# A weight ring of 11 slots in place of 8, square roots in groups of two chunks, and another rstd in the last tile

## The reference

```
xn  = rmsnorm(x);  z = xn @ w_in -> xa, ga, u, v, gates
A:  xc = causal_conv(xa);  r, i = sigmoid(block-diagonal maps of xc)
    log_a = -8 * r * softplus(-lam);  a = exp(log_a);  mult = sqrt(-expm1(2*log_a))
    h = scan(h = a*h + mult*(i*xc));  o_a = (h * gelu(ga)) @ w_br_a
B:  o_b = (gelu(u) * (w_s @ layernorm(gelu(v)) + b_s)) @ w_br_b      (128-position chunks)
mix = (sigmoid(g_a)*o_a + sigmoid(g_b)*o_b) @ w_out;  x += rmsnorm(mix)
f = (silu(gate) * up) @ w_ffn_out, gate/up = rmsnorm(x) @ w_ffn_in;  x += rmsnorm(f)
```

## Time and profile before

| | |
|---|---|
| time, median of 3 runs | 2117.57 us (2116.72 to 2122.35) |
| time of the profiled execution | 2120.24 us |
| its span on the slowest core, core 5 | 2118.5 us |
| spans of the 8 cores | 2103.1 to 2118.5 us |
| TensorE busy on core 5 | 2064.9 us (97%) |
| VectorE, ScalarE, GpSimd busy | 1192.0, 911.3, 359.4 us |
| DMA, mean over the span | 189 GB/s |

### The profile page before, as it was taken

How to read it: one execution, slowest core, us unless ns; L and a number is a source line. 1 busy time by engine, 2 the same in 40 slices (tenths; PEclk the granted TensorE clock), 3 DMA queues, 4 the chain that set the end, 5 groups by cost and what they waited for, 6 DMA issues and landing times.

```text
span 2118.5 us, 34763 instructions; the slowest of 8 cores (2103.1 to 2118.5 us)
## 1 busy us (share of the span) xinstructions
PE 2064.9 (97%) x10771; PEld 1019.9 (48%) x10771; DVE 1192.0 (56%) x1878; ACT 911.3 (43%) x1546; POOL 359.4 (17%) x735
## 2 busy tenths in 40 slices
PE   7999999999999999999999999999999999999997
PEld 3444444444444444444454455445564455445553
DVE  5887488524785257833675168625763587236342
ACT  5667476213761246512752148215822483133111
POOL 3211333113210122001210031003101212121000
PEclk9999999999999999999999999999999999999999
DMA  8655778997478974677554476447666645865652
GB/s 200 140 130 104 206 180 199 186 207 242 159 183 185 236 233 145 184 195 222 199 179 159 153 265 200 159 156 259 210 201 193 230 162 165 257 215 194 212 185 90
DMA packets 113671, 401.43 MB, mean 189 GB/s; under 512 B 14089, under 2 KB 14097, under 8 KB 113490
## 3 DMA queue, kind: packets, MB, share of 16 engines
q1 hardware_dynamic: 96786, 340.43, 48.5%
q0 software_dynamic: 16272, 57.68, 17.1%
q10 hardware_dynamic: 432, 1.09, 0.2%
HBM read 403.26 MB, written 53.54 MB: 216 GB/s over the span
## 4 chain that ended last, share of the span: by engine, by line
PE 89%; DMA 6%; DVE 2%; issue 1%; ACT 1%; SPq 0%; POOL 0%; DVEq 0%; POOLq 0%; ACTq 0%
PE ps L783 62%; PE ps L1376 13%; PE ps L1074 5%; PE ps L1277 5%; DMA wring<-wall 2%; DMA wring<-wsc 2%; PE ps L684 1%; PE ps L964 1%; PE ps L1389 1%; DMA xin<-xp 1%; DVE xcf L946 1%; PE ps L1136 1%; DMA x<-xp 1%; PE ps L1484 0%; DMA yp<-x 0%
## 5 line engine op out<-in xcount | busy, mean ns | idle before, releaser
L783 PE MATMUL ps<-xnT,wring 128*128 128x512 bf16 (+2 forms) x5696 | 1154.3, 359 | 11.7 <-DMA wring<-wall 4.0
L783 PEld LDWEIGHTS ps<-xnT,wring 128*128 128x128 bf16 x5696 | 552.7, 98 | 560.1 <-issue 24.8
L1376 PE MATMUL ps<-wring,ffT 128*128 128x512 bf16 (+1 forms) x1364 | 297.1, 379 | 0.0
L1355 ACT ACTIVATE sgt<-ps 128x512 f32<-128x512 f32 (+2 forms) x198 | 109.4, 555 | 403.4 <-PE ps L783 395.4
L1359 DVE SCALAR_TENSOR_TENSOR sgt<-sgt,ps 128x512 f32<-128x512 f32 (+2 forms) x198 | 125.3, 633 | 213.3 <-PE ps L783 212.9
L1376 PEld LDWEIGHTS ps<-wring,ffT 128*128 128x128 bf16 (+1 forms) x1364 | 132.8, 98 | 162.4 <-issue 4.6
L946 DVE SCALAR_TENSOR_TENSOR xcf<-xa,vecs_sb,xcf 128x512 f32<-128x512 f32 (+2 forms) x240 | 163.4, 681 | 26.7 <-DVE xcf L946 0.9
L1361 DVE SCALAR_TENSOR_TENSOR ffT<-sgt,ps 128x512 bf16<-128x512 f32 (+2 forms) x198 | 125.8, 635 | 39.5 <-PE ps L783 36.4
L500 POOL DMA_DIRECT2D wring<-wall x113 | 63.4, 561 | 445.5 <-PE ps L783 343.4
L656 POOL TENSOR_SCALAR stats<-stats 128x1 f32<-128x1 f32 (+1 forms) x132 | 35.6, 270 | 562.4 <-ACT ffT L669 461.2
L1399 ACT ACTIVATE sgt<-ps 128x512 f32<-128x512 f32 x66 | 38.5, 593 | 197.5 <-PE ps L1376 181.3
(11 more groups left out here) (159 smaller groups left out, 2085.2 us busy)
## 6 DMA issues: line engine op xcount, KB each, us to landing
wring<-wsc SPq DMA_DIRECT2D x473, 512.0 KB, 4.5
wring<-wall POOLq DMA_DIRECT2D x107, 512.0 KB, 9.8
wsc<-wring SPq DMA_DIRECT2D x68, 512.0 KB, 9.4
x<-xp SPq DMA_DIRECT2D x31, 512.0 KB, 7.8
yp<-x SPq DMA_DIRECT2D x29, 512.0 KB, 7.0
xin<-xp SPq DMA_DIRECT2D x28, 512.0 KB, 6.3
wring<-wsc SPq DMA_DIRECT2D x12, 256.0 KB, 3.5
wring<-wall POOLq DMA_DIRECT2D x6, 256.0 KB, 8.5
```

What stands on the lines that cost most here:

```text
L783: mm(lambda e, k=k: e.matmul(ps[:, b, 0:nt], lhsT=wv[:, k, m * 128:(m + 1) * 128], rhs=rhsT[:, k, 0:nt], start=(k == 0), stop=(k == NCH - ...
L1355: act(lambda e: e.activation(out=sgt[:, i, 0:nt], in_=ps[:, b, 0:nt], func=AF.Tanh, scale=0.5), nt, [("ps", b)], [("sgt", i)])
L1376: mm(lambda e, j=j, kk=kk, b=b, PT=PT, col=col: e.matmul(ps[0:PT, b, :], lhsT=ffT[:, j, col:col + PT], rhs=wv[:, kk, :], start=(j == 0), s ...
```

## The change

The ring gets 11 slots, and the scratch area for the DMAs that GpSimd issues is set to 4096 bytes a partition in place of the default. While tile 1's rows are not all squared, at most 8 pieces are loaded ahead. In the pair the 16 places form 8 groups of two square roots, in order of their first place; single tiles keep 4 and 4. In the last tile `fa` adds and takes a reciprocal on VectorE and a square root on ScalarE; the multiplication by the gain becomes a stage of its own, `fg`, after it, and writes to `chE` in place of PSUM.

```diff
-NSLOT = 8
+NSLOT = 11
-    nc = bass.Bass("TRN2", target_bir_lowering=False)
+    nc = bass.Bass("TRN2", target_bir_lowering=False, dynamic_dma_scratch_size=4096)
-                most = 0 if ... else 5 if ("xsq", 0, 3) not in done else len(stream)
+                most = 0 if ... else 5 if ("xsq", 0, 3) not in done else 8 if ("xsq", 1, 3) not in done else len(stream)
+                    if n == "sqrt":
+                        q.extend(sorted(sum(map(list, rest), []), key=lambda z: z.key[2]))
+                        continue
+                sq_from = [0, 2, 4, 6, 8, 10, 12, 14] if M == 2 else [0, 4]
+
                 def sq_of(c):
-                    return -1 if M == 2 and upos(c) < 2 else upos(c) // 4
+                    return max(p for p in sq_from if p <= upos(c))
-                    if upos(c) % 4 == 3 or M == 2 and upos(c) == 1:
-                        put("sqrt", ("sqrt", mem[0], sq_of(c)), lambda c=c: sqrt([GU["ch", i] for i in range(max(0, upos(c) - 3), upos(c) + 1)
-                                                                                   if M == 1 or upos(c) != 3 or i > 1]),
+                    if upos(c) + 1 in sq_from + [M * NCH]:
+                        put("sqrt", ("sqrt", mem[0], sq_of(c)), lambda c=c: sqrt([GU["ch", i] for i in range(sq_of(c), upos(c) + 1)]),
                     ss = sq_half(s, b)
+                    if final:
+                        r = G["fr", s] = stat()
+                        dve(lambda e: e.tensor_scalar(out=stats[0:PT, r:r + 1], in0=stats[0:PT, ss:ss + 1], scalar1=stats[0:PT, G["ss0", s]:G["ss0", s] + 1],
+                                                      scalar2=epsc[0:PT, :], op0=ALU.add, op1=ALU.add), 1, [("st", ss), ("st", G["ss0", s]), ("epsc",)], [("st", r)])
+                        dve(lambda e: e.reciprocal(out=stats[0:PT, r:r + 1], in_=stats[0:PT, r:r + 1]), 1, [("st", r)], [("st", r)])
+                        act(lambda e: e.activation(out=stats[0:PT, r:r + 1], in_=stats[0:PT, r:r + 1], func=AF.Sqrt), 1, [("st", r)], [("st", r)], table="sqrt")
+                        return
+                def fg(s):
+                    PT = T.subs[s][1]
+                    b = B["fo", 1, s]
+                    dve(lambda e: e.tensor_tensor(out=chE[0:PT, s, :], in0=ps[0:PT, b, :], in1=gbc_pf[0:PT, 512:1024], op=ALU.mult), 512,
+                        [("ps", b), ("gbc_pf",)], [("chE", s)])
-                    for n, (src, cell) in ((1, (ps[0:PT, b, :], ("ps", b))), ...
+                    for n, (src, cell) in ((1, (chE[0:PT, s, :], ("chE", s)) if final else (ps[0:PT, b, :], ("ps", b))), ...
+                    if final:
+                        put("fg", ("fg", t, s), lambda s=s: fg(s), needs=ps_of("fo", 1, s), after=[("fa", t, s), ("mix", t, 7)])
-                    put("fb", ..., after=[("fa", t, s)])
+                    put("fb", ..., after=[("fa", t, s)] + ([("fg", t, s)] if final else []))
```

More of the change, by code:

```diff
@@ L511, in fill @@
                 at = P.free["pe"]
-                most = 0 if ("su_zero",) not in done else 3 if ("xsq", 0, 1) not in done else 5 if ("xsq", 0, 3) not in done else len(stream)
+                most = 0 if ("su_zero",) not in done else 3 if ("xsq", 0, 1) not in done else 5 if ("xsq", 0, 3) not in done else 8 if ("xsq", 1, 3) not in done else len(stream)
                 while wo and P.ready([("wr", wo[0])]) <= at and ("xl", 1, 3) in done:
@@ L1421, in fb @@
                     b, r = B["fo", 1, s], G["fr", s]
-                    for n, (src, cell) in ((1, (ps[0:PT, b, :], ("ps", b))), (0, (fh0[0:PT, s, :], ("gvh", s // 2, s % 2)))):
+                    for n, (src, cell) in ((1, (chE[0:PT, s, :], ("chE", s)) if final else (ps[0:PT, b, :], ("ps", b))), (0, (fh0[0:PT, s, :], ("gvh", s // 2, s % 2)))):
                         half = slice(n * 512, (n + 1) * 512)
@@ L1452, in tile_stages @@
                     put("fa", ("fa", t, s), lambda s=s: fa(s), needs=ps_of("fo", 1, s), after=[("fo", t, 6 + s if final else 11), ("ev0", t, s)])
-                    put("fb", ("fb", t, s), lambda s=s: fb(s), needs=lambda s=s: [("st", G["fr", s])], after=[("fa", t, s)])
+                    if final:
+                        put("fg", ("fg", t, s), lambda s=s: fg(s), needs=ps_of("fo", 1, s), after=[("fa", t, s), ("mix", t, 7)])
+                    put("fb", ("fb", t, s), lambda s=s: fb(s), needs=lambda s=s: [("st", G["fr", s])], after=[("fa", t, s)] + ([("fg", t, s)] if final else []))
                     if final:
@@ L1463, in record @@
                 ("act", "pna hna hnb xcb xae gev gex sqrt sig fia ve gae ue xsc xsq fa su_decay su_vin"),
-                ("dve", "hte xte pnb brx fie gin scan cv ln ln2 vb spe ev0 fb su_gates su_spat"),
+                ("dve", "hte xte pnb brx fie gin scan cv ln ln2 vb spe ev0 fb fg su_gates su_spat"),
                 ("pool", "mix init vout su_vecs"),
```

## The result

The changed kernel takes 2090.64 us (median) against 2119.96 us for the kernel before in the same runs, a ratio of 0.9857 with a 95% interval of 0.9829 to 0.9885: about 30 us, or 1.4%, faster.

A forecast was written before the change was run, and what follows sets the result against it. TensorE, busy 2064.9 of 2118.5 us, bounds the kernel, so only its useless time can go. Ring 21.6 + square roots 0 + last tile 0.3 - new plan 2 = 19.9 us; 2100.3, less 2.7, gives 2098 us, range 2085 to 2114.

The forecast's parts named there:

- The ring, 21.6 us: Ring of 11 slots: more lead removes TensorE's waits on ring loads and identity matmuls beside them; 21.6 us, between 0 and 26.1.
- (c): At 517 us: a TensorE wait of 1.89 us on a ring load goes, taken whole.
- (d): From 1641 to 1667 us: 3.7 us in three waits and 3 identity matmuls go, 4.4 us, taken whole.
- (e): From 1862 to 1869 us: 3 identity matmuls, 3.01 us of idleness and 1.2 us of slow matmuls go, 4.9 us.
- (a): From 89 to 98 us: 5 identity matmuls, 3.11 us of idleness and 1.5 us of slow matmuls go, 5.9 us.
- (b): From 300 to 366 us: ring waits and 28 identity matmuls, 8.9 us; half taken, 4.5, as ScalarE may delay next.
- The square roots, 0: Pair's square roots in twos: 3 to 6 more table loads, hidden, against earlier scans; 0 taken, bounds -2 to +7.7 us.
- The new plan, a loss of 2 us within -4 to +8: Planner's order changes everywhere and waits unrelated to the ring are dealt out anew; 2 us charged, between -4 and +8.
- The last tile, 0.3 us by a shorter chain: Last square to line 1424: VectorE and ScalarE replace GpSimd, some 0.9 us for 1.18; 0.3 won, 0.6 won to 0.6 lost.
- Slots opened, not filled: Rival, chance 0.17: the planner opens more stages with the new slots, lead stays one slot; 2113 us, about no change.
- Table switches: Rival, chance 0.10: all six extra ScalarE table loads lie on the path, 7.7 us lost; gain 12.2 us, 2105 us.
- The scratch that holds GpSimd up: Rival, chance 0.09: in bursts of weight loads, GpSimd's issues wait for room in the smaller scratch; slower, 2140 us.

## Why the prediction was right, and which terms were not

Forecast were 19.9 us from the profiled execution and 2098 us; measured were about 30 us and 2090.64. Direction and range (2085 to 2114) hold. Of the cause the ring's part holds in the main, but 5.2 us come from a place that the prediction did not look at, and 8 us or so hang on the plan. That the sum came near the time is in part luck. Term by term:

**What bounds it: right but for the end.** Up to the last matmul only useless time of TensorE went; the stretch from the last output to the last matmul kept its 39.6 us, and the slowest core won more than core 2 (30.7 against 19.9 us).

**The ring, 21.6 us: right in mechanism, too large.** Alone it gave 13.2 us by the stretches' medians, about 15 us by its ratio without the drain. (c), (d) and (e), 11.2 us, were right in sum: after the first output 13.2 us went, and not one ring wait is left there. In the middle stretch 5.4 us went where (c) had 1.9: before, 14 identity matmuls stood there too, 3.0 us, 11 of them just ahead of the wait at 517 us, which (c) left out. (a), 5.9 us, failed. The DMA idleness at 50 us was used as foretold, but TensorE still waits 5.67 us, at 84 us in place of 93; on the other cores this wait was 0 to 1.4 us before and is 0 to 5.0 us now. The chains show the load that it waits for, before and after:

```profile
83.94 9.19 DMA wring<-wall
68.37 15.85 DMA wring<-wall
```

It is issued 15.6 us earlier, as soon as a product at line 1078 has freed a slot, but takes 15.9 us to land in place of 9.2, with the DMA share at 1.01 [window above], and TensorE comes to it 11.5 us earlier (78.8 us in place of 90.3). So the three pieces of lead are used up by 84 us. The step that failed is that three pieces would be enough; with a twelfth slot this wait is all but gone and the stretch to the first output is 6.8 us shorter still. That kernel's plan differs too, and a moved constant alone changes this stretch by 7.9 us, so only the wait itself is shown. (b), taken at half of 8.9 us, was there nearly whole: 8.5 us went between 235 and 440 us with the ring alone. The kernel did not keep it, as the plan for 11 slots is late with the recurrence at 222 us. The prediction's bound of 0 for (b) looked to ScalarE after 300 us; the loss came before.

**The square roots, 0: right alone (0.9995), wrong in the number of loads.** The pair has 6 table loads for square roots, not 8. All table loads rose from 79 to 85, but with the groups as before they are 85 too: the rise comes with the plan for 11 slots, not with the twos. They hide: no wait of TensorE on ScalarE from 45 to 232 us is over 0.5 us, and the kernel without the cap has 5 fewer at the same time. What the prediction did not see is that with 11 slots the plan puts the last square roots later, 221.85 us against 214.10, so that TensorE waits for the recurrence. At that place twos are worth 7.6 us in one plan and 3.6 in another, but in the other nothing of it is left at the first output.

**The new plan, a loss of 2 us within -4 to +8: too narrow.** Moving one constant costs 9.4 us with twos. With fours the medians rise by 3.7 us (2098.91 to 2102.61), but the ratios go the other way (0.9932 and 0.9912, with intervals that overlap), so nothing is shown there. The changed kernel happens on a good plan, which is luck. How its last 8 to 9 us are shared between groups of two and plan stays open: two plans are too few.

**The last tile, 0.3 us by a shorter chain: wrong in place and size.** From the end of the last matmul to line 1424 it was 2.17 us (2106.85 to 2109.02) and is now 2.21; from the add on, 1.18 us became 1.29 in place of 0.9. The last part of the chain of the changed kernel shows it, where line 1441 stands for 1424:

```profile
2073.95 7.47 PE ps L1393 x34
...
2082.34 0.28 DVE stats L1421
...
2082.71 0.16 DVE stats L1423
2082.87 0.60 DVE chE L1433
...
2083.63 0.76 DVE xa L1441
```

The gain multiplication, once beside GpSimd, is now in the chain (0.60 us), which was foretold, and the add takes 0.28 and the reciprocal 0.16 us where 0.1 each was assumed. The 5.2 us after that come from GpSimd's drain. The prediction followed the chain to line 1424 and took what lies behind as fixed; the wait of SyncE at line 330, 5.4 us in the list of waits, stood in the trace and would have told it.

**The rivals.** Slots opened, not filled: wrong, as a limit of 7 pieces held leaves the order as it is. Table switches: six more loads came, and none of their time is seen. The scratch that holds GpSimd up: wrong; it shortens the end.

In sum, by the medians of the stretches: 5.2 us the drain, 14.1 us after the first output, of which the ring alone gives 13.2, and 5.0 us before it, which the ring has only together with the square roots and this plan. On the slowest cores these are 5.3, 17.2 and 8.2 us; the ring alone gives 12.3 of the 17.2 there, and the rest is not given to a cause.

## What to carry to other kernels

A ring that is short of slots loses twice: at the waits that end on its loads, and in filler work that a planner puts where it expects them; count both. Lead won back the waits behind bursts. Where the DMA share is 1.0, three slots of lead only moved the wait, and a fourth removed it; and what lead won in one stage, the new plan lost in another. Follow the chain past the last instruction of the program's own: what the closing barrier waits for can be an engine that did its last small instruction in time. Where a planner makes the order, move one of its constants before a gain of some us is given to an edit, and compare the emitted orders: the run with the limit of 7 turned out to be the changed kernel itself.

## What the runs showed of the hardware that was not expected

GpSimd's closing drain takes 9.9 to 10.4 us in the three kernels with the default scratch area for its DMAs, and 2.3 to 3.3 us in the eleven with 8192 or 4096 bytes, on every core, for the same 113 loads of 9 packets an engine. Where GpSimd works until the end, 5.2 us of the long drain lie on the end. The area itself cost GpSimd's issues nothing (median 528 against 530 ns).
